# A hybrid attention and SwiGLU layer: the down projection's items parted in pairs with twelve raw slots, its last product in PSUM banks of its own

## The chip, the cores and the metric

The kernel runs on one core of one Trainium2 chip. The metric is the device time of one execution in microseconds, the median of several. An engine is named as the profile names it: PE does matrix products, DVE (VectorE) and ACT (ScalarE) elementwise work, POOL (GpSimd) some more of it, SP issues DMAs.

## The reference

One decoder layer on 512 tokens of width 1024, all in float32: a mixer (forgetting attention and sliding window attention, gated and merged), a layer norm, a SwiGLU feed forward of inner width 2816, a second layer norm.

```python
h = layer_norm(alpha * x + mixer(x), ln1_g, ln1_b)
hid = silu(h @ w_gate) * (h @ w_up)          # 512 x 2816
out = layer_norm(alpha * h + hid @ w_down, ln2_g, ln2_b)
```

What is computed here is the last line: a product of 512 x 2816 by 2816 x 1024, added to alpha times the residual, and then normalised over the 1024 channels of each token.

## The kernel before

Every float32 operand is split into a high part (a rounded float32r copy, made by ACT) and a low part (the rest, raw minus high, made by DVE), and each product is three matmuls: high by high, high by low, low by high. The weights of all stages but the last come in 94 slabs of 128x1024. The feed forward's slabs end at slab 94 (`slab_done` counts them), and PE goes straight on to the down projection.

The down projection is one level of a Strassen-like scheme: seven half-size products instead of eight, in the order M5, M1, M3, M6, M2, M7, M4 (`PRODUCTS`, L82). Each product is 11 items (`PAIRS`), so there are 77, numbered 0 to 76; items 55 to 65 are M7 and 66 to 76 are M4. An item takes a 128x256 piece of the activations (`parts`, summed by POOL) and a 128x512 piece of the weights (`wdn`, or `tw` where POOL had made sums of weights ahead). Its way through the engines:

- SP loads the weights into one of four slots of `raw` (L463), once DVE has finished the item four before (`item_ready`).
- ACT makes the high parts: `ah` (128x256, L824), which waits until PE is through with the item eight before (`item_done`, a ring of eight, `RING`), and `sh` (128x512, L826), which waits for the load.
- DVE makes the low parts `al` and `sl` (both L857 by the helper `low`), and counts `item_ready`.
- PE does two blocks of 128 tokens, three matmuls each (L1709 to L1711). With two blocks in turn an item takes PE six matmuls. `item_done` counts after the second block.

Sums of products stay in PSUM: a bank pair BX takes M1, M6, M7 and M4 one on top of the other, BZ M5 and M3, BY M2. What the output needs of them on the way is added to the residual `res` by DVE (`into_residual`, called by `take_bank` and `take_product`; L1297 and L1299), at the item six after the product's end. M4 may go on top of M7 only when DVE has read BX for M7, and PE waits for that (`bank_taken`, 11 + b). M7's last four items and M4's items go block by block (`items_by_block`), so that the first block of each is done earlier (`block0_done`).

The second layer norm goes by blocks of 128 tokens, k = 4 to 7. Blocks 4 and 5 need no M7 and M4 and are normalised by DVE in between the items from item 62 on (`step` in DVE's loop: statistics and variance, the root's start and the first centring, the rest of the root and the second centring, two scalings). ACT takes the square root (`rstd_root`, L694) in its own order behind item 63 and item 68. Blocks 6 and 7 follow after the last item: block 6 while PE does the second block of M4, block 7 behind the last matmul.

All these orders are written out by hand, engine by engine; each engine does its list in order.

Of the kernel before, what the change touches and what calls it, by code (L numbers as in the profile page):

```python
# [24 lines left out]
ALU = mybir.AluOpType  # L25
# [52 lines left out]
BX, BY, BZ = 4, 6, 2  # L78
# [4 lines left out]
            (A22, True, T4, BX, False))  # L83
# [3 lines left out]
DN_RAW = 4  # L87
# [87 lines left out]
def program(nc, xT, x, slabs, vk_slabs, wdn, rope, rope_tok, sel, b_forget, sinks, ln1_g, ln1_b, ln2_g, ln2_b, out):  # L175
    ctx = ExitStack()
    with ctx:
# [16 lines left out]
        al = at("al", 8, [P, RING, 2 * P], F32R)  # L194
        sg = at("sg", 16, [P, 2, SEQ])
# [207 lines left out]
        def item_raw(e):  # L403
            return raw[:, e % DN_RAW * 512:(e % DN_RAW + 1) * 512]

        def item_slot(ring, e):
            return ring[:, item_offset(e):item_offset(e) + 512]
# [4 lines left out]
        def _(sp):  # L412
# [41 lines left out]
            for e in range(ITEMS):  # L454
                p, i = divmod(e, PAIRS)
                _, summed, w, _, _ = PRODUCTS[p]
                if e == 0:
                    sp.wait_ge(t_stored, 16 * PAIRS)
                if e < DN_RAW:
                    sp.wait_ge(lo_ready, ready(N_DN - 2) + e // 2)  # L460
                else:
                    sp.wait_ge(item_ready, e - DN_RAW + 1)
                sp.dma_start(item_raw(e), (tw if summed else wdn)[i, w]).then_inc(item_landed[e % DN_RAW], 16)  # L463
# [105 lines left out]
        def _(act):  # L569
# [238 lines left out]

            def item_split(e):

                p, i = divmod(e, PAIRS)
                if e == 0:
                    act.wait_ge(t_stored, 16 * PAIRS)
                if p == M5:
                    act.wait_ge(part_made, 3 * i + 1)
                if e == M1 * PAIRS:
                    act.wait_ge(part_made, 3 * PAIRS)
                if p == M3:
                    act.wait_ge(s3_made, i + 1)
                if e < RING:  # L820
                    act.wait_ge(slab_done, N_DN - SPL + 1 + e // 2)
                else:
                    act.wait_ge(item_done, e - RING + 1)
                act.activation(ah[:, e % RING, :], item_part(e), ACT.Copy)  # L824
                act.wait_ge(item_landed[e % DN_RAW], 16 * (e // DN_RAW + 1))
                act.activation(item_slot(sh, e), item_raw(e), ACT.Copy).then_inc(item_hi, 1)  # L826

            for r in range(4):
                if r % 2:
                    f = FT - 2 + r // 2  # L830
                    act.wait_ge(ff_done, f - 1)
                    silu(f)
                item_split(2 * r)
                item_split(2 * r + 1)
            for e in range(RING, ITEMS):
                item_split(e)
# [8 lines left out]
        def _(dve):  # L845
# [457 lines left out]
            def take_bank(p, b):  # L1303
# [25 lines left out]
            for r in range(4):  # L1329
# [3 lines left out]
                item_low(2 * r + 1)  # L1333
            for e in range(RING, ITEMS):
                item_low(e)
                if e <= M7 * PAIRS + RING - 2 and e % PAIRS == RING - 2 and e > PAIRS:
                    take_product(e // PAIRS - 1)
                if e == M4 * PAIRS + 3:
                    dve.wait_ge(block0_done, 1)
                    take_bank(M7, 0)  # L1340
                    dve.wait_ge(item_done, PAIRS * (M7 + 1))
                    take_bank(M7, 1)
                    for k in (TB + 2, TB + 3):
                        taken_statistics(k, 1, 9 + k - TB)
                for k in (TB, TB + 1):
# [11 lines left out]
                    elif step in (3, 4):  # L1357
                        scale(k, step - 3)
            k = TB + 2
            dve.wait_ge(block0_done, 2)  # L1360
            take_bank(M4, 0)
            variance(k, taken_statistics(k, 0, 13))
# [5 lines left out]
            variance(k, taken_statistics(k, 0, 14))  # L1368
# [4 lines left out]
        def _(pe):  # L1373
# [312 lines left out]
            def item(p, i, b):  # L1686
# [10 lines left out]
                if i == 0:  # L1697
# [9 lines left out]
                    elif p == M4:  # L1707
                        pe.wait_ge(bank_taken, 11 + b)
# [5 lines left out]
                elif i == PAIRS - 1 and p in (M7, M4):  # L1714
# [96 lines left out]
```

## Time and profile before

| | |
|---|---|
| median of three runs | 705.03 us (704.56 to 705.15) |
| the profiled execution | 705.2 us |
| its span | 703.4 us, so 1.8 us lie around it |
| PE busy | 689.1 us (98%) |
| DVE busy | 431.3 us (61%) |
| ACT busy | 336.7 us (48%) |
| POOL busy | 141.3 us (20%) |
| span's mean granted clock of PE | 0.996 |

The down projection begins at 586.39 us of the span and its last matmul starts at 695.17 us. Matmuls are pipelined: a matmul's row shows 0.39 us, and the next starts 0.23 us after it. DVE and ACT rows overlap in the same way by 0.1 us or less, so what an instruction costs in a row of them is the distance from start to start.

### The profile page before, as it was taken

How to read it: one execution, taken by the hardware profiler on the slowest of the kernel's cores; microseconds unless marked ns; L12 is line 12 of the kernel's file. 1: busy time of each engine (PE TensorE's matmuls, PEld its weight loads, DVE VectorE, ACT ScalarE, POOL GpSimd, SP SyncE). 2: the span in 40 equal slices, each digit the busy share in tenths (PEclk: the TensorE clock that was granted, in tenths of full speed). 3: DMA queues.
4: the chain of work that ended last, by engine and by line, in shares of the span. 5: the costliest groups of instructions: out<-in, count | busy, mean ns of one | idle time of the engine just before them, and what ended most of it. 6: DMA issues, size and time to landing. Idle time of an engine off the chain costs nothing.

```text
span 703.4 us, 9442 instructions
## 1 busy us (share of the span) xinstructions
PE 689.1 (98%) x3380; PEld 577.2 (82%) x3380; DVE 431.3 (61%) x739; ACT 336.7 (48%) x624; POOL 141.3 (20%) x129
## 2 busy tenths in 40 slices
PE   8999999999999999999999999999999999999985
PEld 6987888888888888888998888888888888888873
DVE  5569997767876236647923442233334337989897
ACT  5678787467766344333223222222222225677741
POOL 2110000000001000000236664355533415100000
PEclk9999999999999999999999999999999999999998
DMA  8221112211114522361357556654466433676643
GB/s 320 78 92 61 61 62 89 90 61 61 61 61 133 226 90 91 114 215 61 102 188 248 210 209 217 230 197 154 161 233 209 149 106 103 184 221 211 187 126 135
DMA packets 34723, 102.09 MB, mean 145 GB/s; under 512 B 3584, under 2 KB 3712, under 8 KB 34688
## 3 DMA queue, kind: packets, MB, share of 16 engines
q1 hardware_dynamic: 27504, 74.36, 31.8%
q0 software_dynamic: 7184, 27.27, 11.7%
q8 instruction: 20, 0.33, 0.2%
q14 instruction: 15, 0.12, 0.1%
HBM read 87.99 MB, written 13.63 MB: 144 GB/s over the span
## 4 chain that ended last, share of the span: by engine, by line
PE 88%; DVE 5%; ACT 3%; issue 1%; DMA 1%; POOL 0%; SPq 0%; DVEq 0%
PE ps L1376 22%; PE ps L1378 22%; PE ps L1377 22%; PE ps L1709 4%; PE ps L1711 4%; PE ps L1710 4%; PE ps L1458 2%; PE ps L1444 2%; PE ps L1414 1%; ACT rope L593 1%; DVE sl L857 1%; PE ps L1409 1%; DMA x_raw<-in_xT 1%; PE ps L1419 1%; DVE sl L849 1%
## 5 line engine op out<-in xcount | busy, mean ns | idle before, releaser
L857 DVE TENSOR_TENSOR sl<-raw,sh 128x512 fp32r<-128x512 f32 (+1 forms) x113 | 111.8, 989 | 77.2 <-ACT sh L807 77.2
L1376 PE MATMUL ps<-hTh,sh 128*128 128x512 f32 x320 | 124.5, 389 | 0.0
L1377 PE MATMUL ps<-hTh,sl 128*128 128x512 f32 x320 | 124.5, 389 | 0.0
L1378 PE MATMUL ps<-hTl,sh 128*128 128x512 f32 x320 | 124.5, 389 | 0.0
L807 ACT ACTIVATE sh<-raw 128x1024 fp32r<-128x1024 f32 x36 | 38.2, 1062 | 146.3 <-PE ps L1378 127.6
L849 DVE TENSOR_TENSOR sl<-raw,sh 128x1024 fp32r<-128x1024 f32 x50 | 61.8, 1236 | 54.7 <-ACT sh L577 54.5
L1376 PE MATMUL ps<-xh,sh 128*128 128x512 f32 x208 | 83.7, 403 | 0.0
L1378 PE MATMUL ps<-xl,sh 128*128 128x512 f32 x208 | 81.3, 391 | 0.0
L1377 PE MATMUL ps<-xh,sl 128*128 128x512 f32 x208 | 81.1, 390 | 0.0
L577 ACT ACTIVATE sh<-raw 128x1024 fp32r<-128x1024 f32 x50 | 52.8, 1058 | 42.8 <-PE ps L1378 36.4
L1378 PEld LDWEIGHTS ps<-hTl,sh 128*128 128x128 f32 x320 | 60.1, 188 | 12.6
L1377 PEld LDWEIGHTS ps<-hTh,sl 128*128 128x128 f32 x320 | 60.1, 188 | 12.5
L1376 PEld LDWEIGHTS ps<-hTh,sh 128*128 128x128 f32 x320 | 60.1, 188 | 12.3
L1709 PE MATMUL ps<-sh,ah 128*128 128x512 f32 x154 | 60.6, 393 | 2.7 <-DVE res L1297 1.9
L1711 PE MATMUL ps<-sl,ah 128*128 128x512 f32 x154 | 59.9, 389 | 0.0
L1710 PE MATMUL ps<-sh,al 128*128 128x512 f32 x154 | 59.9, 389 | 0.0
L826 ACT ACTIVATE sh<-raw 128x512 fp32r<-128x512 f32 x77 | 48.2, 625 | 24.4 <-DMA raw<-in_wdn 13.6
L1378 PEld LDWEIGHTS ps<-xl,sh 128*128 128x128 f32 x208 | 39.0, 188 | 8.5
L857 DVE TENSOR_TENSOR al<-parts,ah 128x256 fp32r<-128x256 f32 x77 | 36.0, 467 | 15.9 <-ACT sh L826 15.6
L1377 PEld LDWEIGHTS ps<-xh,sl 128*128 128x128 f32 x208 | 39.2, 188 | 7.0
L1376 PEld LDWEIGHTS ps<-xh,sh 128*128 128x128 f32 x208 | 39.2, 188 | 6.9
L1276 DVE TENSOR_TENSOR parts<-sg,ps 128x512 f32 x18 | 12.4, 688 | 48.0 <-PE ps L1378 48.0
(217 smaller groups left out, 1297.3 us busy)
## 6 DMA issues: line engine op xcount, KB each, us to landing
raw<-in_slabs SPq DMA_DIRECT2D x86, 512.0 KB, 3.3
stage<-in_wdn POOLq DMA_DIRECT2D x11, 1024.0 KB, 9.1
tw<-tsum POOLq DMA_DIRECT2D x11, 1024.0 KB, 5.7
raw<-tw SPq DMA_DIRECT2D x44, 256.0 KB, 2.8
raw<-in_wdn SPq DMA_DIRECT2D x33, 256.0 KB, 2.9
x_raw<-in_xT SPq DMA_DIRECT2D x8, 256.0 KB, 6.1
res<-in_x POOLq DMA_DIRECT2D x1, 2048.0 KB, 8.9
late_raw<-in_slabs SPq DMA_DIRECT2D x4, 512.0 KB, 4.2
```

What stands on the lines that cost most here:

```text
L577: act.activation(slot(sh, n, width_of(n)), raw_of(n), ACT.Copy).then_inc(hi_ready, 1)
L807: act.activation(slot(sh, m), raw_of(m), ACT.Copy).then_inc(hi_ready, 1)
L826: act.activation(item_slot(sh, e), item_raw(e), ACT.Copy).then_inc(item_hi, 1)
L849: dve.tensor_tensor(slot(sl, n, w), raw_of(n), slot(sh, n, w).bitcast(F32), ALU.subtract).then_inc(lo_ready, 1)
L857: return dve.tensor_tensor(dst, src, hi.bitcast(F32), ALU.subtract)
L1376: pe.matmul(dst, lh, rh, start=start, stop=False)
L1377: pe.matmul(dst, ll, rh, start=False, stop=False)
L1378: return pe.matmul(dst, lh, rl, start=False, stop=stop)
L1444: last = pe.transpose(ps[:, 5 + col // 512, col % 512:col % 512 + P], prob[:, off + (kb - k0) * P:off + (kb - k0 + 1) * P], ident[:, :])
L1709: pe.matmul(dst, lh, rh, start=start, stop=False, skip_group_check=True)
L1710: pe.matmul(dst, ll, rh, start=False, stop=False, skip_group_check=True)
L1711: last = pe.matmul(dst, lh, rl, start=False, stop=stop, skip_group_check=True)
```

## The change

Four things, all in the down projection.

- Items are split in pairs (0 and 1, 2 and 3, ...). ACT makes `ah` of both in one instruction and `sh` of both in one; DVE the same for `al` and `sl`. Where a pair straddles two products (10 and 11, 32 and 33, 54 and 55) `ah` and `al` stay separate. A pair's first instruction waits for all that both items need, and its semaphores count by two. Item 76 is alone.
- The raw weights get twelve slots: the four of `raw` and eight in a new tile `dn_raw` at 32 KB, where the transposed hidden input lay, free once slab 94 is done. From item 20 on a load waits for the item twelve before.
- M4 starts fresh in banks of its own (BW = 0), so PE waits for no bank there. M7's bank pair is therefore added to the residual twice per block (subtracted on the right half, added on the left), and M4's is added to the left half: two more DVE instructions in all. M7 is taken at item 72, like every product at the item six after its end. It was taken at item 69 before.
- M7's last four items and M4's first four go block by turn again, and only M4's last seven block by block. The statistics of the right halves of blocks 6 and 7 move from behind item 69 to behind the last item.

Its core (waits of the loads and the ACT side's order behind the pair are as described):

```diff
-BX, BY, BZ = 4, 6, 2
+BX, BY, BZ, BW = 4, 6, 2, 0
 ...
-            (A22, True, T4, BX, False))
+            (A22, True, T4, BW, True))
-DN_RAW = 4
+DN_RAW = 12
+        dn_raw = at("dn_raw", 32, [P, 8 * 512])
 ...
+        def raw_slot(e):
+            return 8 + e % 4 if e < 8 else (e - 8) % DN_RAW
 ...
-                if e < DN_RAW:
+                if e < 4:
                     sp.wait_ge(lo_ready, ready(N_DN - 2) + e // 2)
-                else:
+                elif e < 8:
+                    sp.wait_ge(item_ready, e - 3)
+                elif e == 8:
+                    sp.wait_ge(slab_done, N_DN)
+                elif e >= 8 + DN_RAW:
                     sp.wait_ge(item_ready, e - DN_RAW + 1)
+                elif e >= 16:
+                    sp.wait_ge(item_ready, e - 11)
 ...
             def item_split(e):
+                s = e % RING
+                if e + 1 < ITEMS and one_product(e):
+                    part_free(e, e + 2)
+                    act.activation(ah[:, s:s + 2, :], item_parts(e), ACT.Copy)
 ...
+                count = min(2, ITEMS - e)
+                for m in range(e, e + count):
+                    act.wait_ge(item_landed[raw_slot(m)], 16 * raw_uses(m))
+                act.activation(item_slot(sh, e, count), item_raw(e, count), ACT.Copy).then_inc(item_hi, count)
 ...
             def item_low(e):
-                dve.wait_ge(item_hi, e + 1)
-                low(al[:, e % RING, :], item_part(e), ah[:, e % RING, :])
-                low(item_slot(sl, e), item_raw(e), item_slot(sh, e)).then_inc(item_ready, 1)
+                s = e % RING
+                count = min(2, ITEMS - e)
+                dve.wait_ge(item_hi, e + count)
+                if count == 2 and one_product(e):
+                    low(al[:, s:s + 2, :], item_parts(e), ah[:, s:s + 2, :])
+                else:
+                    for m in range(e, e + count):
+                        low(al[:, m % RING, :], item_part(m), ah[:, m % RING, :])
+                low(item_slot(sl, e, count), item_raw(e, count), item_slot(sh, e, count)).then_inc(item_ready, count)
 ...
                 elif p == M7:
                     into_residual(2 + b, 1, BX + b, ALU.subtract, 1 + b)
+                    into_residual(2 + b, 0, BX + b, ALU.add, 0)
                 else:
-                    into_residual(2 + b, 0, BX + b, ALU.add, 0)
+                    into_residual(2 + b, 0, BW + b, ALU.add, 12 + 2 * b)
 ...
             for e in range(RING, ITEMS):
-                item_low(e)
-                if e <= M7 * PAIRS + RING - 2 and e % PAIRS == RING - 2 and e > PAIRS:
+                if e % 2 == 0:
+                    item_low(e)
+                if e % PAIRS == RING - 2 and e > PAIRS:
                     take_product(e // PAIRS - 1)
-                if e == M4 * PAIRS + 3:
-                    dve.wait_ge(block0_done, 1)
-                    take_bank(M7, 0)
 ...
                     elif p == M7:
                         pe.wait_ge(bank_taken, 7 + b)
-                    elif p == M4:
-                        pe.wait_ge(bank_taken, 11 + b)
 ...
-            for p in range(M7):
+            for p in range(M4):
                 for i in range(PAIRS):
                     items_by_block(p, i, i + 1)
-            for i in range(PAIRS - DN_TAIL):
-                items_by_block(M7, i, i + 1)
-            items_by_block(M7, PAIRS - DN_TAIL, PAIRS)
-            items_by_block(M4, 0, DN_TAIL)
+            for i in range(DN_TAIL):
+                items_by_block(M4, i, i + 1)
             items_by_block(M4, DN_TAIL, PAIRS)
```

DVE's list where the normalisation of block 4 begins, before: L857 is a low part, first that of item 62's weights; L1105 the variance, L1114 to L1128 the root, L1136 a centring, L1154 a scaling.

```order
L857 TENSOR_TENSOR sl<-raw,sh 128x512
L1327 BN_STATS stats<-res 128x6 [waits bank_taken] x2
L1105 BN_AGGR mv<-stats 128x2 [waits ln_part]
L857 TENSOR_TENSOR al<-parts,ah 128x256 [waits item_hi]
L857 TENSOR_TENSOR sl<-raw,sh 128x512
L1114 TENSOR_SCALAR rstd<-mv 128x1 [waits ln_var,ln_right,ln_left]
L1136 SCALAR_TENSOR_TENSOR res<-res,mv,ln2p 128x512 [waits ln2_landed]
L857 TENSOR_TENSOR al<-parts,ah 128x256 [waits item_hi]
L857 TENSOR_TENSOR sl<-raw,sh 128x512
L1120 RECIPROCAL rstd<-rstd 128x1 [waits ln_root]
L1123 TENSOR_SCALAR rstd<-rstd 128x1 [waits ln_half,ln_rec]
L1136 SCALAR_TENSOR_TENSOR res<-res,mv,ln2p 128x512 [waits ln2_landed]
```

The same place of the changed kernel, from the low part of the pair of items 62 and 63 (its weights). L900 is the low part, L1157 to L1171 the root, L1179 the centring, L1197 the scaling.

```order
L900 TENSOR_TENSOR sl<-dn_raw,sh 128x1024
L1377 BN_STATS stats<-res 128x6 [waits bank_taken] x2
L1148 BN_AGGR mv<-stats 128x2 [waits ln_part]
L1157 TENSOR_SCALAR rstd<-mv 128x1 [waits ln_var,ln_right,ln_left]
L1179 SCALAR_TENSOR_TENSOR res<-res,mv,ln2p 128x512 [waits ln2_landed]
L900 TENSOR_TENSOR al<-parts,ah 128x512 [waits item_hi]
L900 TENSOR_TENSOR sl<-raw,sh 128x1024
L1163 RECIPROCAL rstd<-rstd 128x1 [waits ln_root]
L1166 TENSOR_SCALAR rstd<-rstd 128x1 [waits ln_half,ln_rec]
L1179 SCALAR_TENSOR_TENSOR res<-res,mv,ln2p 128x512 [waits ln2_landed]
L1171 TENSOR_SCALAR rstd<-rstd 128x1 [waits ln_newton]
L1197 SCALAR_TENSOR_TENSOR res<-res,rstd,ln2p 128x512 [waits ln_rstd,ln_centred_l]
```

The low part that stood between the variance and the root's start is gone into the pair ahead of them, and the root's last step is now followed by the scaling that needs it.

DVE's list where M7 is taken, before: it begins at item 69's low part; L1297 adds or subtracts a bank to the residual.

```order
L857 TENSOR_TENSOR al<-parts,ah 128x256 [waits item_hi]
L857 TENSOR_TENSOR sl<-raw,sh 128x512
L1297 TENSOR_TENSOR res<-res,ps 128x512 [waits bank_taken,block0_done]
L1297 TENSOR_TENSOR res<-res,ps 128x512 [waits bank_taken,item_done]
L1327 BN_STATS stats<-res 128x6 [waits bank_taken] x2
L1120 RECIPROCAL rstd<-rstd 128x1 [waits ln_root]
L1123 TENSOR_SCALAR rstd<-rstd 128x1 [waits ln_half,ln_rec]
```

And in the changed kernel, from the pair of items 72 and 73 to that of 74 and 75. L1346 and L1348 are the four additions of M7's banks.

```order
L900 TENSOR_TENSOR al<-parts,ah 128x512 [waits item_hi]
L900 TENSOR_TENSOR sl<-dn_raw,sh 128x1024
L1346 TENSOR_TENSOR res<-res,ps 128x512 [waits bank_taken,item_done]
L1348 SCALAR_TENSOR_TENSOR res<-res,ps 128x512 [waits ln_left]
L1346 TENSOR_TENSOR res<-res,ps 128x512 [waits bank_taken]
L1348 SCALAR_TENSOR_TENSOR res<-res,ps 128x512 [waits ln_left]
L900 TENSOR_TENSOR al<-parts,ah 128x512 [waits item_hi]
L900 TENSOR_TENSOR sl<-dn_raw,sh 128x1024
```

The taking moved from behind item 69 to behind item 73, and went from two instructions to four; the statistics (L1327) that followed it are not here any more.

PE's list at the first matmuls of M4, before (ahead of them the second block of M7's last items):

```order
L1709 MATMUL ps<-sh,ah 128x512
L1710 MATMUL ps<-sh,al 128x512
L1711 MATMUL ps<-sl,ah 128x512
L1709 MATMUL ps<-sh,ah 128x512 [waits bank_taken,item_ready]
L1710 MATMUL ps<-sh,al 128x512
L1711 MATMUL ps<-sl,ah 128x512
L1709 MATMUL ps<-sh,ah 128x512 [waits item_ready]
```

The same rows of the list in the changed kernel:

```order
L1752 MATMUL ps<-sh,ah 128x512
L1753 MATMUL ps<-sh,al 128x512
L1754 MATMUL ps<-sl,ah 128x512
L1752 MATMUL ps<-sh,ah 128x512 [waits item_ready]
L1753 MATMUL ps<-sh,al 128x512
L1754 MATMUL ps<-sl,ah 128x512
L1752 MATMUL ps<-sh,ah 128x512
```

The wait for the bank is gone, and PE waits for the parts of an item (`item_ready`) at every other block, since the two blocks of an item now follow each other.

## Rows read from the trace of the kernel before

**Rows 1.** Page, part 4: shares of the chain that ended last, by engine

```profile
PE 88%; DVE 5%; ACT 3%; issue 1%; DMA 1%; POOL 0%; SPq 0%; DVEq 0%
```

**Rows 2.** Waits by engine, 655 to 703.4 us: total, times, longest (us)

```profile
ACT sh L826 <- DMA raw<-tw: 6.3, 7, 2.3
...
PE ps L1709 <- DVE res L1297: 1.9, 1, 1.9
```

**Rows 3.** Timeline, PE, from 586 us: start us, us, engine line op

```profile
586.39 0.39 PE L1709 MATMUL ps<-sh,ah 128*128 128x512 f32 x1
...
675.93 0.39 PE L1711 MATMUL ps<-sl,ah 128*128 128x512 f32 x1
678.19 0.47 PE L1709 MATMUL ps<-sh,ah 128*128 128x512 f32 x1 [1.88 <-DVE res L1297]
...
689.83 0.50 PE L1709 MATMUL ps<-sh,ah 128*128 128x512 f32 x1 [0.87 <-DVE sl L857]
...
695.17 0.39 PE L1711 MATMUL ps<-sl,ah 128*128 128x512 f32 x1
```

**Rows 4.** Timeline, ACT, 660 to 667 us

```profile
660.03 0.42 ACT L824 ACTIVATE ah<-parts 128x256 fp32r<-128x256 f32 x1 [0.42 <-PE ps L1711]
...
665.84 0.40 ACT L824 ACTIVATE ah<-parts 128x256 fp32r<-128x256 f32 x1
666.15 0.62 ACT L826 ACTIVATE sh<-raw 128x512 fp32r<-128x512 f32 x1
666.68 0.40 ACT L824 ACTIVATE ah<-parts 128x256 fp32r<-128x256 f32 x1
```

**Rows 5.** Timeline, DVE, 661.9 to 671.5 us

```profile
661.95 1.28 DVE L1297 TENSOR_TENSOR res<-res,ps 128x512 f32<-128x512 f32 x2
663.14 0.42 DVE L857 TENSOR_TENSOR al<-parts,ah 128x256 fp32r<-128x256 f32 x1
...
664.08 1.28 DVE L1327 BATCH_NORM_STATS2 stats<-res 128x6 f32<-128x512 f32 x2
...
665.52 0.37 DVE L857 TENSOR_TENSOR al<-parts,ah 128x256 fp32r<-128x256 f32 x1
...
666.41 0.15 DVE L1114 TENSOR_SCALAR rstd<-mv 128x1 f32<-128x1 f32 x1
...
667.14 0.42 DVE L857 TENSOR_TENSOR al<-parts,ah 128x256 fp32r<-128x256 f32 x1
...
668.07 0.15 DVE L1120 RECIPROCAL rstd<-rstd 128x1 f32<-128x1 f32 x1
...
669.24 0.42 DVE L857 TENSOR_TENSOR al<-parts,ah 128x256 fp32r<-128x256 f32 x1
...
670.17 0.75 DVE L1154 SCALAR_TENSOR_TENSOR res<-res,rstd,ln2p 128x512 f32<-128x512 f32 x1
670.83 0.42 DVE L857 TENSOR_TENSOR al<-parts,ah 128x256 fp32r<-128x256 f32 x1
```

**Rows 6.** Timeline, DVE, item 76's last low part, and two rows of block 6

```profile
689.09 0.69 DVE L857 TENSOR_TENSOR sl<-raw,sh 128x512 fp32r<-128x512 f32 x1
...
694.40 0.21 DVE L1128 TENSOR_SCALAR rstd<-rstd 128x1 f32<-128x1 f32 x1
694.71 0.75 DVE L1154 SCALAR_TENSOR_TENSOR res<-res,rstd,ln2p 128x512 f32<-128x512 f32 x1
```

**Rows 7.** Timeline, ACT and DVE, one 128x1024 weight slab

```profile
532.19 1.06 ACT L807 ACTIVATE sh<-raw 128x1024 fp32r<-128x1024 f32 x1 [3.89 <-PE ps L1378]
...
533.29 1.23 DVE L857 TENSOR_TENSOR sl<-raw,sh 128x1024 fp32r<-128x1024 f32 x1 [0.30 <-ACT sh L807]
```

**Rows 8.** Timeline, DVE and POOL, 590 to 602 us

```profile
593.58 0.95 DVE L857 TENSOR_TENSOR al<-parts,ah 128x256 fp32r<-128x256 f32 x1
...
595.60 0.95 DVE L857 TENSOR_TENSOR al<-parts,ah 128x256 fp32r<-128x256 f32 x1
...
590.28 10.93 POOL L563 TENSOR_TENSOR parts<-parts 128x256 f32<-128x256 f32 x11
```

More of the change, by code:

```diff
@@ L401, in item_part, with raw_uses, item_raw, item_slot @@
             return parts[:, i, PRODUCTS[p][0] * 2 * P:(PRODUCTS[p][0] + 1) * 2 * P]
[L403 to L407, printed above, removed]
+        def raw_slot(e):
+            return 8 + e % 4 if e < 8 else (e - 8) % DN_RAW
+        def raw_uses(e):
+            if e < 8:
+                return e // 4 + 1
+            return (e - 8) // DN_RAW + (3 if raw_slot(e) >= 8 else 1)
+        def item_raw(e, count=1):
+            r = raw_slot(e)
+            if r >= 8:
+                return raw[:, (r - 8) * 512:(r - 8 + count) * 512]
+            return dn_raw[:, r * 512:(r + count) * 512]
+        def item_slot(ring, e, count=1):
+            return ring[:, item_offset(e):item_offset(e) + 512 * count]
+        def item_parts(e):
+            p, i = divmod(e, PAIRS)
+            return parts[:, i:i + 2, PRODUCTS[p][0] * 2 * P:(PRODUCTS[p][0] + 1) * 2 * P]
+        def one_product(e):
+            return e // PAIRS == (e + 1) // PAIRS
         block = ctx.enter_context(nc.Block())
@@ L807, in _, with part_free @@
                     act.activation(slot(sh, m), raw_of(m), ACT.Copy).then_inc(hi_ready, 1)
-            def item_split(e):
[L811 to L821, printed above, removed]
-                else:
[L823 to L826, printed above, removed]
+            def part_free(e, end):
+                for e in range(e, end):
+                    p, i = divmod(e, PAIRS)
+                    if e == 0:
+                        act.wait_ge(t_stored, 16 * PAIRS)
+                    if p == M5:
+                        act.wait_ge(part_made, 3 * i + 1)
+                    if e == M1 * PAIRS:
+                        act.wait_ge(part_made, 3 * PAIRS)
+                    if p == M3:
+                        act.wait_ge(s3_made, i + 1)
+                    if e < RING:
+                        act.wait_ge(slab_done, N_DN - SPL + 1 + e // 2)
+                    else:
+                        act.wait_ge(item_done, e - RING + 1)
@@ new lines, in item_split @@
+            def item_split(e):
+                s = e % RING
+                if e + 1 < ITEMS and one_product(e):
+                    part_free(e, e + 2)
+                    act.activation(ah[:, s:s + 2, :], item_parts(e), ACT.Copy)
+                else:
+                    part_free(e, e + 1)
+                    act.activation(ah[:, s, :], item_part(e), ACT.Copy)
+                    if e + 1 < ITEMS:
+                        part_free(e + 1, e + 2)
+                        act.activation(ah[:, s + 1, :], item_part(e + 1), ACT.Copy)
+                count = min(2, ITEMS - e)
+                for m in range(e, e + count):
+                    act.wait_ge(item_landed[raw_slot(m)], 16 * raw_uses(m))
+                act.activation(item_slot(sh, e, count), item_raw(e, count), ACT.Copy).then_inc(item_hi, count)
@@ L1358, in _ @@
                         scale(k, step - 3)
+            for k in (TB + 2, TB + 3):
+                taken_statistics(k, 1, 11 + 2 * (k - TB - 2))
             k = TB + 2
-            dve.wait_ge(block0_done, 2)
+            dve.wait_ge(block0_done, 1)
             take_bank(M4, 0)
-            variance(k, taken_statistics(k, 0, 13))
+            variance(k, taken_statistics(k, 0, 15))
             centre_both(k)
@@ L1367, in _ @@
             take_bank(M4, 1)
-            variance(k, taken_statistics(k, 0, 14))
+            variance(k, taken_statistics(k, 0, 16))
             centre_both(k)
@@ L1713, in item @@
                     last.then_inc(item_done, 1)
-                elif i == PAIRS - 1 and p in (M7, M4):
+                elif i == PAIRS - 1 and p == M4:
                     last.then_inc(block0_done, 1)
```

12 lines of the change are left out of this document (4 added, 8 removed).

## The prediction

> **What bounds the kernel now.** First the chain of waits that ended last, in shares by engine: 88% of it is PE [rows 1]. Nothing that another engine does counts unless it makes PE wait or lies behind its last matmul. Second, PE's timeline over the down projection: do its matmuls follow each other without a hole? The first starts at 586.39, and the last of item 65 at 675.93, after which the next could start 0.23 later, at 676.16. That is 89.77 us for 66 items, 1.36 us an item, 0.68 a block, with nothing lost. All 77 items would end at 586.39 + 77 x 1.36 = 691.11. The last matmul starts at 695.17, so they end at 695.40 [rows 3]. PE lost 4.29 us, all behind item 65. That is the most the change can win here: 705.03 - 4.3 = 700.7.
>
> Third, who PE waited for. 2.03 of the 4.29 go at M4's first matmul (676.16 to 678.19), where DVE had not yet read M7's bank [rows 2, 3]. The other 2.26 lie between 678.2 and 690.6, in small steps at the blocks of M4's last seven items, each released by a low part from DVE, the largest at 689.83 [rows 3]. In that part PE takes a new item every 0.68 us and DVE needs 0.94 for one (663.14 to 664.08) [rows 5]. Fourth, therefore, DVE's timeline: from 661.95 on it does the takings and the normalisation of blocks 4 and 5 between the items [rows 5].
>
> **The change, part by part.** Prices are distances from start to start.
>
> The bank wait goes: 2.03 us, with certainty, since M4 has its own banks. But a wait that goes only counts if the next item is ready. What is late next is DVE's low part, so DVE's list has to be walked through.
>
> Prices for that. An instruction on 128x512 costs 0.60 (two takings, 661.95 to 663.14, make 1.19). A 128x1024 low part lasts 1.23 in its row [rows 7]. A row on 128x512 lasts 0.75 while the next starts after 0.66, an overhang of 0.09 [rows 5], so it costs 1.14. A pair then costs 0.60 + 1.14 = 1.74, against 2 x 0.94 = 1.88 before, 0.14 saved. The bounds of that term: 1.88 if joining saves nothing; below, 256 columns more cost 0.60 - 0.34 = 0.26 and a pair has six times 256, so 1.56 if the fixed part vanished altogether. I take 1.74, the nearest row. On ACT the pair's activations take 0.53, as a 128x512 copy does (666.15 to 666.68) [rows 4], and DVE starts 1.10 after the 128x1024 copy does (532.19 to 533.29) [rows 7].
>
> The walk, from the last point that PE sets in both kernels. ACT's copy at 660.03 waited for item 53's end [rows 4] (586.39 + 54 x 1.36 = 659.83, and the last row's overhang). Before, that released item 61. Now it releases the pair 60 and 61, since a pair needs the ring free for its second item. DVE starts at 660.03 + 0.53 + 1.10 = 661.66. Pair 60/61 to 663.40 (item 61 alone was done at 661.95 [rows 5]). M2's takings 1.19: 664.59. Pair 62/63: 666.33. Statistics and variance 1.44 (664.08 to 665.52 [rows 5]): 667.77.
>
> Here a new hole opens. ACT takes the root only after the variance, and copies after that: before, its next copy stood 0.32 behind the variance's end (665.52 to 665.84 [rows 4, 5]). Before, item 63 filled DVE in this gap and item 64 alone came soon. Now items 64/65 reach DVE at 667.77 + 0.32 + 0.53 + 1.10 = 669.72, and DVE has only the root's start and a centring for that time, 0.73 (666.41 to 667.14 [rows 5]). About 1.0 us of DVE is idle in its busiest stretch.
>
> Pair 64/65: 671.46. Rest of the root with a centring 1.17 (668.07 to 669.24): 672.63. The scaling 0.66 (670.17 to 670.83 [rows 5]) now follows the root's last step at once and waits for it: in block 6 that step and the scaling lie 0.31 apart, against a row of 0.21 that others overlap [rows 6]; I put 0.12 on it: 673.41. Pair 66/67: 675.15. Scaling: 675.81. Statistics of block 5: 677.25. Pair 68/69: 678.99. Its root and centrings in one piece, 0.73 + 1.17: 680.89. Pair 70/71: 682.63. Two scalings: 683.95. Pair 72/73: 685.69. M7's takings, four where there were two, 4 x 0.60: 688.09. Pair 74/75: 689.83.
>
> PE's side. A low part's start and the matmul it releases are 0.74 apart (689.09 [rows 6] to 689.83 [rows 3]), which is 0.60 and 0.14. So PE can start item 74 at 689.97. Without any wait it would have got there at 586.39 + 70 x 1.36 + 4 x 0.68 = 684.31. It has 5.66 us of waits up to this point, spread over items 68 to 74, the largest (over 2 us) at item 74 behind M7's takings. From there it has three blocks of the first and seven of the second kind: 10 x 0.68, and 0.13 for the restart (689.83 to 695.40 is 8 x 0.68 + 0.13 [rows 3]), end at 696.90. Against 695.40: **1.5 us later**. In one sentence: PE resumes for the last time at about the same moment as before, but with ten blocks to do instead of eight.
>
> The rest of the change. Item 76 and the moved statistics end by 689.83 + 0.94 + 1.20 = 691.97, before or at the first block's end (about 692.1), so block 6 fits into the second block's 4.76 us as before; if not, some tenths. The loads: eight start at slab 94 instead of one by one behind DVE, and from item 20 on each has twelve items' time, 16 us; ACT waited 6.3 us for loads in the last 48 us before [rows 2], and that goes. It gains nothing by itself, as DVE's list above never waits for a load. Behind the last matmul nothing changes: one addition, block 7, the store.
>
> POOL's eleven sums, 10.93 us from 590.28, slow DVE: an item's low parts cost 2.02 instead of 0.94 (593.58 to 595.60) [rows 8], 0.54 for each of two instructions. If it is by instruction, a pair costs 1.74 + 1.08 = 2.82 against PE's 2.72: harmless in seven pairs with some 3 us in hand. If it grows with size, a pair costs 4.04 and item 10 is ready at about 586.39 + 0.2 + 1.63 + 3 x 4.04 = 600.3 and a restart later, against 600.0: up to 0.6 us late, which goes straight through: PE is shifted by it. I take the first, at nothing, since 0.54 is the same for both sizes within the sum.
>
> Sum against the profiled execution: span 703.4 + 1.5 = 704.9, and the 1.8 around it, 706.7; its time was 0.2 above the median, so 705.03 + 1.5 = **706.5**.
>
> A rule that speaks against the change: the Trainium skill (Perfetto Trace Analysis, Optimizing Scalar/DVE Operations) says that grouping into larger operations helps where the engine is saturated, but where Scalar or Vector are not saturated and yet cause bubbles elsewhere, breaking instructions up lets work be done sooner. Its first half would make the change a gain of 0.14 a pair, its second half a loss of a pair's delay. DVE here is both, full behind 661.95 and with gaps ahead of it; the rows give the delay (1.45 us at pair 60/61) as larger than the eight savings of 0.14.
>
> **Rivals.** *The waits simply go* (chance 0.12): M7's bank wait was 2.03, the loads kept ACT waiting 6.3 us, both are cured, and PE loses little: between 700.7 and 703.4, say 702.3. For it: both waits stand in the profile by name. Against: DVE has no hole between 661.95 and item 73's low parts, so there is little for faster loads to fill. It decides if DVE has item 74 ready more than 3 us earlier than reckoned, that is with no hole at the root and M7's takings beside something.
>
> *Joining saves more than the rows say* (0.21): a pair costs 1.60, and eight of them give back 1.1 us; the loss and the gain cancel, 705.4.
>
> *POOL's contention grows with size* (0.10): item 10 late, 706.5 + 0.6 = 707.1, with PE holes near 600.
>
> *The forecast* (0.55), by its own bounds 705.8 (pairs at 1.66) to 707.6 (pairs at 1.88). The other 0.02: eight loads at once delay item 8, or PE's clock falls in the holes.
>
> **How the numbers follow.** About 0.2%, 1.4 us, is what a measurement of this kernel can tell from no change: 703.6 and 706.4 are the borders. Faster: the first rival, 0.12. Within: the second, 0.21, and 0.15 of the forecast's 0.55, whose lower part ends below 706.4: 0.36. Slower: 0.40 of the forecast, 0.10 and 0.02: 0.52. The range, 703.4 to 708.4, leaves out most of the first rival below and a forecast that errs together with the third above. The forecast's own range is 705.8 to 707.6.
>
> **What would show it.** No PE wait at M4's first matmul for a bank, but waits for DVE's low parts at items 68, 70, 72 and, the longest, 74, over 5 us together. ACT never waiting for a load behind 620. DVE with one hole of about 1 us behind the first centring near 668.7, and full from there to item 76. Low parts on 128x1024 at 1.23. Last matmul start at about 696.7. Wrong if PE's holes sum to less than 4.3 us, if item 74's low parts end before 688, or if PE waits between 590 and 620.

## The result, and the profile after

The changed kernel takes 707.2 us, the median of ten runs (705.57 to 709.8). The kernel before, beside it on the same chip, takes 705.04 (704.56 to 706.66). The ratio is 1.003, with a 95% interval of 1.002 to 1.0039: about 2.2 us slower. The profiled execution is the fastest of the ten: 705.57 us, with a span of 703.8. So it shows the change at its mildest, which turns out to matter.

The chain of waits by engine, part 4 of the page of the changed kernel, answers to [rows 1]:

```profile
PE 88%; DVE 5%; ACT 3%; issue 2%; DMA 1%; POOL 0%; DVEq 0%; SPq 0%; ACTq 0%
```

PE is still the bound. Its waits, and those it hangs on, from 655 to 703.8 us (total, times, longest), against [rows 2]:

```profile
ACT rstd L721 <- DVE mv L1148: 20.0, 4, 11.0
...
PE ps L1752 <- DVE sl L900: 4.5, 3, 2.5
DVE al L900 <- ACT sh L869: 3.8, 4, 1.1
ACT ah L859 <- PE ps L1754: 3.4, 3, 1.1
```

ACT's 6.3 us for loads are gone and so is PE's 1.9 for a bank. In their place PE waits 4.5 for low parts. PE's timeline, against [rows 3]. This execution reaches the first item's matmul at 585.39, the one before at 586.39, so times are compared from there:

```profile
678.17 0.50 PE L1752 MATMUL ps<-sh,ah 128*128 128x512 f32 x1
...
681.80 0.50 PE L1752 MATMUL ps<-sh,ah 128*128 128x512 f32 x1 [0.61 <-DVE sl L900]
...
684.86 0.50 PE L1752 MATMUL ps<-sh,ah 128*128 128x512 f32 x1 [1.40 <-DVE sl L900]
...
688.99 0.50 PE L1752 MATMUL ps<-sh,ah 128*128 128x512 f32 x1 [2.47 <-DVE sl L900]
...
695.68 0.39 PE L1754 MATMUL ps<-sl,ah 128*128 128x512 f32 x1
```

Items 68, 70, 72 and 74 start late. From the first item's matmul to the last matmul's start is 695.68 - 585.39 = 110.29 us. Before it was 695.17 - 586.39 = 108.78. I call this the stretch; it grew by 1.51. The span grew only from 703.4 to 703.8, since the first item came 1.00 earlier here. Over the fourteen traces of this document that moment lies between 585.39 and 586.39, and it differs by 0.46 even between single_items and single_late, whose programs are the same up to there. So the stretch, and not the span, is compared between traces. Item 74 would have started at 585.39 + 97.92 = 683.31 without waits, and starts 5.68 late.

DVE's timeline, against [rows 5 and 6]:

```profile
660.70 0.69 DVE L900 TENSOR_TENSOR al<-parts,ah 128x512 fp32r<-128x512 f32 x1 [0.89 <-ACT sh L869]
661.31 1.22 DVE L900 TENSOR_TENSOR sl<-dn_raw,sh 128x1024 fp32r<-128x1024 f32 x1
662.45 1.28 DVE L1346 TENSOR_TENSOR res<-res,ps 128x512 f32<-128x512 f32 x2
...
667.11 0.74 DVE L1179 SCALAR_TENSOR_TENSOR res<-res,mv,ln2p 128x512 f32<-128x512 f32 x1
668.74 0.69 DVE L900 TENSOR_TENSOR al<-parts,ah 128x512 fp32r<-128x512 f32 x1 [0.89 <-ACT sh L869]
...
671.53 0.21 DVE L1171 TENSOR_SCALAR rstd<-rstd 128x1 f32<-128x1 f32 x1
671.84 0.75 DVE L1197 SCALAR_TENSOR_TENSOR res<-res,rstd,ln2p 128x512 f32<-128x512 f32 x1
...
684.73 0.68 DVE L1346 TENSOR_TENSOR res<-res,ps 128x512 f32<-128x512 f32 x1
...
686.52 0.68 DVE L1348 SCALAR_TENSOR_TENSOR res<-res,ps 128x512 f32<-128x512 f32 x1
687.12 0.68 DVE L900 TENSOR_TENSOR al<-parts,ah 128x512 fp32r<-128x512 f32 x1
687.72 1.22 DVE L900 TENSOR_TENSOR sl<-dn_raw,sh 128x1024 fp32r<-128x1024 f32 x1
688.85 0.42 DVE L900 TENSOR_TENSOR al<-parts,ah 128x256 fp32r<-128x256 f32 x1
```

A pair takes 0.61 + 1.14 = 1.75. DVE is done with pair 60/61 at 662.45, stands idle for 0.97 before 668.74, is full from there, and gives 2.39 us to four takings of M7 (684.73 to 687.12) before the last pair.

### The profile page after: what moved, and what is told of

The parts are those of the page before. It is cut to its first block, busy times and chain, and to the rows that moved or that the text cites. A ratio compares the mean times of both kernels' runs of the same rounds, so it can differ in the third digit from the quotient of the medians.

```text
span 703.8 us, 9359 instructions
## 1 busy us (share of the span) xinstructions
PE 688.6 (98%) x3380; PEld 577.4 (82%) x3380; DVE 429.0 (61%) x668; ACT 327.0 (46%) x551; POOL 144.8 (21%) x129
## 4 chain that ended last, share of the span: by engine, by line
PE 88%; DVE 5%; ACT 3%; issue 2%; DMA 1%; POOL 0%; DVEq 0%; SPq 0%; ACTq 0%
PE ps L1421 22%; PE ps L1423 22%; PE ps L1422 22%; PE ps L1752 4%; PE ps L1753 4%; PE ps L1754 4%; PE ps L1503 2%; PE ps L1489 2%; DVE sl L900 1%; PE ps L1459 1%; PE ps L1454 1%; ACT rope L620 1%; PE ps L1464 1%; DMA first_raw<-in_slabs 1%; DVE sl L892 1%
## 5 line engine op out<-in xcount | busy, mean ns | idle before, releaser
L900 DVE TENSOR_TENSOR sl<-raw,sh 128x1024 fp32r<-128x1024 f32 (+1 forms) x51 | 76.3, 1497 | 76.9 <-ACT sh L834 76.9
L900 DVE TENSOR_TENSOR al<-parts,ah 128x512 fp32r<-128x512 f32 (+1 forms) x42 | 30.5, 732 | 23.8 <-ACT sh L869 23.8
L859 ACT ACTIVATE ah<-parts 128x512 fp32r<-128x512 f32 x35 | 22.1, 631 | 44.2 <-PE ps L1754 29.2
```

The costliest lines, as they stand in the source:

```text
L859: act.activation(ah[:, s:s + 2, :], item_parts(e), ACT.Copy)
L900: return dve.tensor_tensor(dst, src, hi.bitcast(F32), ALU.subtract)
```

## The experiments

Each was timed beside the kernel before, in three groups. The median of before was 705.00 in the first (again, slots_only, single_items, late_take), and on another chip 705.29 in the second (banks_only, single_late, mixed_late, filled) and 705.39 in the third (pairs_to_61, root_later, two_takings, before_filled). So between groups ratios to before are compared, not times. A ratio's 95% interval is about 0.001 to each side, 0.6 to 0.8 us. The theory: DVE's list sets the end of the down projection, by three delays (joining at pair 60/61, the hole at the root, two more takings ahead of the last pair), and the loads are worth nothing. What it did not cover at first is why the median is 2.2 us above before and the stretch only 1.5. The interval of the ratio begins at 1.4 us, so this 0.7 is itself uncertain.

**again**: the changed kernel, unchanged.

> The changed kernel as it is, once more, for its spread and a second trace. Its median was 2.2 us above before, 0.7 us more than the 1.5 us that its own trace shows between the first item and the last matmul (110.29 against 108.78 us). Theory A (the whole loss lies in the down projection, the rest is scatter of the first 15 us, where the loads of the input arrive): the stretch from the first item's matmul to the last matmul is 110.3 us again within 0.3, and the median stands 1.0 to 2.2 above before. Rival (the change costs something more, in the stretch too, in some executions): the stretch differs by over 0.5 from the first trace.

707.53 us (706.34 to 708.15), ratio 1.0033 (1.0021 to 1.0045). The second trace, timeline of PE behind the last hole:

```profile
689.19 0.50 PE L1752 MATMUL ps<-sh,ah 128*128 128x512 f32 x1 [2.47 <-DVE sl L900]
...
690.26 0.63 PE L1752 MATMUL ps<-sh,ah 128*128 128x512 f32 x1
690.68 0.63 PE L1753 MATMUL ps<-sh,al 128*128 128x512 f32 x1
...
692.82 0.51 PE L1752 MATMUL ps<-sh,ah 128*128 128x512 f32 x1
693.16 0.39 PE L1753 MATMUL ps<-sh,al 128*128 128x512 f32 x1
...
697.50 0.39 PE L1754 MATMUL ps<-sl,ah 128*128 128x512 f32 x1
```

and PE in windows of the same trace (from:to, length, busy and matmuls, granted clock, DMA share, GB/s):

```profile
685.00:690.00 5.00, 2.47 (x9) 0.96 0.00 0
690.00:692.00 2.00, 2.00 (x7) 0.50 0.00 0
692.00:694.00 2.00, 2.00 (x8) 0.73 0.00 0
```

The holes are the same (0.61, 1.40, 2.47), but behind the last one the granted clock is 0.50, the 1.2 GHz level, for some 3 us. Seven steps from matmul to matmul are 0.43 instead of 0.23, and the two around them 0.1 too long: 7 x 0.2 + 0.2 = 1.6 us. The stretch is 697.50 - 585.60 = 111.9, so 1.6 longer. In the first trace all these windows have 1.00. So the rival was right here: the change costs more in some executions, in the stretch itself, by the clock behind the holes. The medians agree with that as the source of the 0.7 us, though a second trace alone doesn't prove it; filled tests it below.

**slots_only**: before, with twelve raw slots.

```diff
-DN_RAW = 4
+DN_RAW = 12
```

> The kernel before with the twelve raw slots alone: items one at a time, M4 on top of M7 with its bank wait. Theory (DVE bounds the end, loads cost PE only the one hole ahead of item 76): ACT waits for no load behind 600 us, the bank wait stays at about 1.9, holes behind it shrink by 0.9: time 0.9 below before, stretch 107.9. Rival (the load waits of 6.3 us were a cause of their own): 2 us or more below before. Second rival (loads were hidden anyway): same as before.

704.39 us (703.62 to 705.14), 0.9988 (0.9978 to 0.9998). The stretch is 108.23, 0.55 shorter than before. What went is before's hole of 0.87 ahead of item 76 [rows 3], where ACT had waited 0.93 for item 76's load (ACT's timeline of before):

```profile
688.08 0.63 ACT L826 ACTIVATE sh<-raw 128x512 fp32r<-128x512 f32 x1 [0.93 <-DMA raw<-tw]
```

The bank's hole is still there, and the clock is lowered behind it (PE's timeline, then a window, then DVE's timeline at item 76):

```profile
678.08 0.63 PE L1725 MATMUL ps<-sh,ah 128*128 128x512 f32 x1 [1.88 <-DVE res L1313]
...
680.64 0.63 PE L1725 MATMUL ps<-sh,ah 128*128 128x512 f32 x1
681.07 0.63 PE L1726 MATMUL ps<-sh,al 128*128 128x512 f32 x1
```

```profile
680.00:685.00 5.00, 5.00 (x20) 0.84 0.15 56
```

```profile
688.08 0.68 DVE L873 TENSOR_TENSOR sl<-raw,sh 128x512 fp32r<-128x512 f32 x1
```

Eight steps of 0.43 from 678.08 to 681.50 make about 1.6 us of lost clock, yet the stretch is only 0.3 above the 107.9 expected. DVE starts item 76's low part at 688.08, so PE, 0.74 later as in before, could not have begun that item ahead of 688.82, however fast its matmuls; it began at 689.30. Most of what PE lost was time in which it would have waited for DVE. Slow matmuls cost their full length only if no such wait follows them.

**single_items**: the changed kernel with items one at a time (twelve slots, own banks, four takings stay). **banks_only**: the same with four slots.

```diff
+SIZE = {e: 1 for e in range(ITEMS)}
 ...
-                count = min(2, ITEMS - e)
+                count = SIZE[e]
```

> The changed kernel with items parted one at a time; twelve slots, M4's own banks and the four takings stay. Theory (pairs cost: the delay of a pair, the hole at the root, and two more blocks behind the last low part): walked through with the prices of the trace, PE's last low parts come one by one, holes of about 2.5 us at item 73 behind M7's takings and small ones after, last matmul 2.3 us earlier than in the changed kernel: stretch 107.9 us, time 0.9 us below before. Rival (the two more takings are the cause, pairs help by 0.14 each): 0.5 to 1 us above the changed kernel, stretch about 111.

> The changed kernel with items one at a time and four raw slots: M4's own banks, the four takings and the new block order alone. Theory (with own banks the loads aren't on DVE's path): the same as the single kernel with twelve slots, 704.5, hole of 2.3 to 2.5 at item 73. Rival (the loads then set the last items, as they did before the change ahead of item 76): 0.5 to 1.5 us more than that.

704.47 (703.43 to 706.64), 0.9992 (0.9984 to 1.0001), and 704.78 (703.8 to 705.91), 0.9993 (0.9984 to 1.0002). The stretches are 109.0 and 109.03. Each has a single hole, at item 73, the first behind M7's takings here (PE's timeline of the first, its window, and DVE's low part of item 76):

```profile
685.61 0.50 PE L1757 MATMUL ps<-sh,ah 128*128 128x512 f32 x1 [2.30 <-DVE sl L903]
```

```profile
685.00:690.00 5.00, 4.39 (x11) 0.66 0.00 0
```

```profile
687.68 0.68 DVE L903 TENSOR_TENSOR sl<-raw,sh 128x512 fp32r<-128x512 f32 x1
```

The walk gave 107.9 for the first. The trace agrees: DVE starts item 76's low part at 687.68, so PE could begin that item at 688.42, and eight blocks and a restart behind it the last matmul would start at 693.76, a stretch of 107.9. The other 1.1 us is the clock behind the hole (0.66). Two things follow. With banks of their own for M4, slots are worth nothing that these intervals show. And joining, the only thing left out, is what costs: without it the other edits are not measurably slower than before.

**pairs_to_61**: pairs for items 0 to 61, one at a time after.

```diff
+SIZE = {e: 2 if e < 62 else 1 for e in range(ITEMS) if e >= 62 or e % 2 == 0}
```

> The changed kernel with pairs only for items 0 to 61, before the normalisation, and single items from 62 on. M4's own banks, twelve slots and four takings stay. Theory (a pair's delay at the point where DVE becomes the bound costs most): item 61's low parts end 1.45 us later than with single items, and this is never made up: stretch 109.4 us in an execution that keeps its clock, 1.4 above the single kernel's 107.9 without clock loss; median 705.5 to 706.2, the single kernel's being 704.5. Rival (only the pairs during the normalisation cost, by the hole at the root and the late last items): same as the single kernel.

706.26 (705.04 to 707.12), 1.0011 (1.0002 to 1.002), stretch 110.15. PE's timeline:

```profile
682.50 0.50 PE L1757 MATMUL ps<-sh,ah 128*128 128x512 f32 x1 [0.27 <-DVE sl L903]
...
684.10 0.50 PE L1757 MATMUL ps<-sh,ah 128*128 128x512 f32 x1 [0.64 <-DVE sl L903]
...
687.43 0.80 PE L1757 MATMUL ps<-sh,ah 128*128 128x512 f32 x1 [2.37 <-DVE sl L903]
```

It differs from single_items only in how DVE comes into its busy part, one pair against single items. The hole at 687.43 is again ahead of item 73, which starts 687.43 - 586.18 = 101.25 behind the first item, against 685.61 - 585.87 = 99.74: 1.51 later, ahead of any lowered clock. That is the delay at pair 60/61, predicted as 1.45, and it is never made up. The stretch shows 1.15 of it, since single_items lost 1.1 to the clock behind its hole and pairs_to_61, by the same reckoning from its item 76, 0.75. The ratios show 1.3, with 0.9 to each side.

**root_later**: ACT's roots and DVE's root steps each a pair later, so that a pair stands in the hole.

```diff
+STEPS = {62: ((4, 0),), 63: ((4, 1),), 66: ((4, 2), (4, 3)), 67: ((4, 4), (5, 0)), 68: ((5, 1),),
+         70: ((5, 2),), 71: ((5, 3), (5, 4))}
 ...
-                    if e == M7 * PAIRS + RING + 5 * (k - TB):
+                    if e == M7 * PAIRS + RING + 2 + 4 * (k - TB):
```

> The changed kernel with ACT's square roots one pair later (behind items 65 and 69) and DVE's rest of the root behind items 67 and 71: pairs throughout. Theory (DVE's hole of about 0.9 us between the first centring and pair 64/65 goes, since ACT splits 64/65 before it takes the root): stretch 109.4 us, 0.8 to 0.9 below the changed kernel in an execution that keeps its clock; median 0.5 to 1 below it. Rival (the hole only absorbs what DVE would wait for later): stretch 110.3.

706.62 (704.99 to 707.38), 1.002 (1.0012 to 1.0029). DVE's timeline has no hole now:

```profile
667.33 0.74 DVE L1181 SCALAR_TENSOR_TENSOR res<-res,mv,ln2p 128x512 f32<-128x512 f32 x1
667.98 0.69 DVE L902 TENSOR_TENSOR al<-parts,ah 128x512 fp32r<-128x512 f32 x1
```

The stretch is 109.51, 0.8 shorter where the hole was 1.0. PE's timeline shows why the clock has no part in the difference:

```profile
685.67 0.63 PE L1753 MATMUL ps<-sh,ah 128*128 128x512 f32 x1
686.10 0.63 PE L1754 MATMUL ps<-sh,al 128*128 128x512 f32 x1
...
688.43 0.50 PE L1753 MATMUL ps<-sh,ah 128*128 128x512 f32 x1 [1.27 <-DVE sl L902]
```

The clock falls behind the hole of 1.97 ahead of item 72 (0.72 in the window from 685), but item 74 waits for DVE after that, and starts 688.43 - 585.60 = 102.83 behind the first item against 103.60. DVE is 0.77 earlier and not 0.97, since the second root's last step is now followed by its scaling too and waits for it, 0.31 where it took 0.13. By ratio the kernel is 0.7 us below the changed one, inside the expected 0.5 to 1, but the two intervals overlap, and it stays above before. The delay exists; curing it alone doesn't undo the loss.

**two_takings**: M7's banks are added to only one half, which leaves two additions out of the result.

```diff
-                    into_residual(2 + b, 0, BX + b, ALU.add, 0)
```

> The changed kernel without the two additions of M7's banks to the left half of the residual (that part of the sum is left out). Theory (each instruction of DVE ahead of the last pair costs its 0.60 in full): stretch 109.1 us, 1.2 below the changed kernel in an execution that keeps its clock, hole at item 74 of 1.3 instead of 2.5; median 1.0 to 1.8 below it. Rival (they lie in DVE's slack): same as the changed kernel.

704.75 (704.05 to 706.8), 0.9994 (0.9985 to 1.0002). PE's timeline at item 74, and stretch 109.11:

```profile
688.08 0.50 PE L1751 MATMUL ps<-sh,ah 128*128 128x512 f32 x1 [1.27 <-DVE sl L900]
```

Two takings are 1.20, and the hole went from 2.47 to 1.27, as expected. The median went down by more than the 1.0 to 1.8 expected, 0.36% or 2.5 us against the changed kernel (0.9 to each side). The granted clock of this trace stays 1.00. That a hole half as long costs less than half would fit; with one trace it isn't shown.

**late_take**: the changed kernel with M7's takings behind item 76.

```diff
-                if e % PAIRS == RING - 2 and e > PAIRS:
+                if e % PAIRS == RING - 2 and e > PAIRS and e // PAIRS - 1 != M7:
 ...
+            take_product(M7)
```

> The changed kernel with M7's four takings moved from behind item 73 to behind item 76. Theory (DVE's list is the bound and what is moved behind the last low part comes back ahead of block 6): PE's hole at item 74 falls from 2.5 to about 0.3 and its last matmul comes 2.4 us earlier (stretch 107.9), but block 6's normalisation then starts 2.0 us after its block is done and block 7's waits for it: only 0.5 us below the changed kernel. Rival (PE's last matmul sets the end): 2.4 us below the changed kernel.

705.74 (705.19 to 706.16), 1.0008 (0.9999 to 1.0017). PE keeps the two small holes (0.61 and 1.40) and the clock; the stretch is 107.91, 2.4 shorter. Yet the span is 703.8, as in the changed kernel's trace: from the last matmul's start to the span's end it is now 9.93 us instead of 8.12, since DVE, with the takings still to do, sets the end, and the other 0.6 is a later first item (585.96). So 1.8 of the 2.4 us came back behind PE. By ratio the kernel is 1.6 us below the changed one, more than the expected 0.5, and its eleven executions lie within 1.0 us: the hole at item 74, behind which the clock could fall, is gone.

**single_late**: late_take with single items. **mixed_late**: the same, but pairs for items 66 to 73 alone, in DVE's full part, where each saves 0.14.

```diff
+SIZE = {e: 2 if 66 <= e < 74 else 1 for e in range(ITEMS) if not (66 <= e < 74 and e % 2)}
```

> The same with every item alone. Theory: 0.6 us above the mixed kernel (four pairs save 0.14 each), 1.0 below before, clock at 1.00 and a narrow spread, while the kernel with single items and the takings at item 72 had a hole of 2.3 us, a granted clock of 0.66 behind it and stood only 0.5 below before. Rival (the place of the takings doesn't matter in the single kernel, since DVE sets the end in both): same median as that kernel, 704.5.

> The changed kernel with items one at a time, pairs only from item 66 to 73, where ACT is ahead and a pair delays nothing, and M7's takings behind item 76. Theory (DVE's list sets the end, PE holes over some 1.5 us also cost clock in some executions): PE has one hole of about 0.3 us, its clock stays at 1.00, the last matmul comes at a stretch of about 105 us, DVE ends the kernel: 1.5 us below before in the walk, and 1.5 to 2.3 in the median, since before has a hole of 1.88 that can cost clock. Rival (holes don't matter, PE's last matmul sets the end): 4 us below before. Second rival (takings behind item 76 cost more than they give, as in the run with pairs): same as before.

703.97 (703.28 to 704.3), 0.9981 (0.9972 to 0.999), and 703.42 (702.58 to 704.95), 0.9979 (0.9969 to 0.9989). The traces list no wait of PE for DVE in either. Mixed_late's windows (same columns) are all but full until its last matmul, and its stretch is 104.94, hardly more than 77 x 1.36 = 104.72; single_late's is 105.51, so four pairs save 0.57, about 4 x 0.14, though the two times can't be told apart:

```profile
680.00:685.00 5.00, 4.93 (x22) 1.00 0.28 105
685.00:690.00 5.00, 5.00 (x23) 1.00 0.00 0
690.00:692.00 2.00, 0.74 (x4) 1.00 0.00 0
```

Of 3.84 us of stretch saved against before, 1.5 (by ratio) to 1.9 (by medians) remain in the time, since part of block 6 and block 7 now wait for DVE behind the last matmul: from its start to the span's end it is 700.7 - 690.35 = 10.35 us, against 703.4 - 695.17 = 8.23 before. Both versions stand below before with their whole intervals, and so below the changed kernel.

**filled**: the changed kernel, with useless matmuls in the holes.

```diff
+FILL = {M4 * PAIRS + 4: 2, M4 * PAIRS + 6: 5, M4 * PAIRS + 8: 10}
 ...
+                    for _ in range(FILL.get(e, 0)):
+                        pe.matmul(ps[:, BY, :], ah[:, (e - 1) % RING, 0:P], item_slot(sh, e - 1), start=True, stop=True,
+                                  skip_group_check=True)
                     pe.wait_ge(item_ready, e + 1)
```

> The changed kernel with matmuls of no use put into PE's three last holes: two ahead of item 70, five ahead of 72, ten ahead of 74, into a bank that nothing reads any more, all shorter than the holes. The output's work is unchanged. Theory (in some executions the granted clock falls behind the holes and the last blocks go at 0.43 us a matmul, which is the 0.7 us between the trace's 1.5 and the median's 2.2, and the wide spread): stretch 110.3 us in every execution, clock 1.00 to the last matmul, median 0.5 to 1.0 below the changed kernel and spread under 1.5 us. Rival (scatter comes from the first 15 us): same median and spread as the changed kernel.

705.92 (705.55 to 706.78), 1.0013 (1.0004 to 1.0022). The work is more and items 70, 72 and 74 start as late as without them (item 70 at 682.41, 96.40 behind the first item, against 681.80 - 585.39 = 96.41; item 74 at 103.59 against 103.60). The stretch is 110.3 with the clock at 1.00, and the median is 1.2 us lower than the changed kernel's by ratio (0.9 to each side). The spread is 1.2 us, against 4.2 in the ten executions of the changed kernel and 1.8 in the six of again. What differs is PE's idle time, so some of the changed kernel's time hangs on it: by this run 1.2 us, by the stretch 0.7.

**before_filled**: the same for before, eight ahead of M4's first matmul and three ahead of item 76.

```diff
+                        for _ in range(8):
+                            pe.matmul(ps[:, BY, :], lh, rh, start=True, stop=True, skip_group_check=True)
```

> The kernel before with matmuls of no use in its holes: eight ahead of M4's first matmul, where PE waits for the bank, three ahead of item 76. The output's work is unchanged. Theory (before too loses clock behind its hole of 1.9 us in some executions): 0.3 to 0.8 us below before, stretch 108.8 us. With it the loss by the walk alone can be read between two kernels that keep their clock: the filled changed kernel (705.92) should stand 1.5 above this one, so 704.4. Rival (before loses no clock): same as before, and the two stand 0.6 to 0.9 apart.

705.51 (704.35 to 706.52), 1.0003 (0.9994 to 1.0012), stretch 108.95. I expected 0.3 to 0.8 below before; nothing came. The rival, that before loses next to nothing by the clock, fits, and slots_only shows a likely reason: behind the bank's hole DVE sets the pace and slow matmuls cost little. No trace of before itself has a lowered clock there, so this is argued. Filled should then stand 1.35 to 1.5 above this kernel (the stretches are 110.30 and 108.95), and by ratio it stands 0.7 above, with 0.9 to each side. So the two don't contradict each other, and they don't settle the size either.

## Why the prediction was right, and which term was mis-sized

706.5 was predicted, 707.2 measured, inside the range and slower by over 0.2% as the likeliest case had it. The forecast's 1.5 us is not met by luck: the steps that it is made of came out one by one.

- *The bank wait goes, low parts take its place*: shown in the trace of after (no wait for a bank, 4.5 us for low parts).
- *The walk*: from ACT's copy for pair 60/61 (ACT's timeline of the changed kernel, against [rows 4])

```profile
659.09 0.63 ACT L859 ACTIVATE ah<-parts 128x512 fp32r<-128x512 f32 x1 [1.14 <-PE ps L1754]
```

  to PE's end I had 36.87 us. In the trace it is 695.68 + 0.23 - 659.09 = 36.82. The takings ahead of the last pair, 2.39 against 2.40, and the start of item 74 (5.68 behind an unhindered PE against 5.66) came out as reckoned. "1.5 us later" is 1.51 between the two traces.
- *The delay at pair 60/61*: 1.45 reckoned, 1.51 between pairs_to_61 and single_items at item 73.
- *A pair costs 1.74*: 1.75. The rival that joining saves more falls, and so does the one that the waits simply go.
- *The loads gain nothing*: banks_only and single_items agree within 0.0001 in ratio. In the old order of the blocks and banks they were worth something: slots_only has a stretch 0.55 shorter and a ratio just below 1, since item 76's load came late before.
- *The hole at the root*: 0.97 against 1.0; root_later closed it and had item 74 start 0.77 earlier.
- *The scaling waits for the root's last step*: 671.53 to 671.84, 0.31, as reckoned.
- *POOL slows DVE by instruction, not by size*: settled by the trace. Pairs beside POOL's sums, DVE's timeline and POOL's row, against [rows 8]:

```profile
588.45 1.75 DVE L900 TENSOR_TENSOR sl<-raw,sh 128x1024 fp32r<-128x1024 f32 x1
590.14 1.21 DVE L900 TENSOR_TENSOR al<-parts,ah 128x512 fp32r<-128x512 f32 x1
591.28 1.76 DVE L900 TENSOR_TENSOR sl<-dn_raw,sh 128x1024 fp32r<-128x1024 f32 x1
```

```profile
589.21 14.68 POOL L590 TENSOR_TENSOR parts<-parts 128x256 f32<-128x256 f32 x11
```

  The pair takes 591.28 - 590.14 = 1.14 and 592.96 - 591.28 = 1.68, so 0.54 more for either size, 2.82 in all. PE waits for nothing there.
- *PE's clock falls in the holes*: this was the mis-sized term. The prediction named it among "the other 0.02" and gave it no price. In the traces it costs 1.6 us in one execution (again), nothing in another (after), and by the medians 0.7 to 1.2: the changed kernel loses 2.2 where its stretch in the mildest execution loses 1.5, and filled is 1.2 below it. The ten executions of the changed kernel fit: the two slowest (709.43 and 709.8) have the lowest mean granted clock, 0.993, and the two with the highest, 0.998, took 706.54 and 705.88. But the slowest stand 4 us above the traced one, more than the 1.6 that a trace shows, and none of them was traced; what else they lost stays open. The holes could be seen ahead: the change turns small steps of 2.26 in all and one wait of 2.03 into three real holes that grow, 0.61, 1.40 and 2.47, close together, the last with no wait behind it that would take up slow matmuls. Only the trace of before, at 1.00 behind its own hole, spoke for no cost. The Trainium skill (TensorE: Matmul & The Clock Gate, A second HAM failure mode: psum-queue depth-cycling) says that frequent micro-idles between groups of matmuls make the clock swing between its two levels, and that it is the swing that costs throughput. By that sentence the forecast would have been above 706.5, and the traces of again (0.50), root_later (0.72) and pairs_to_61 (0.73) agree that the clock falls, while those of after and two_takings, at 1.00, show that it need not. Single_items (0.66) has but one hole, so it doesn't take several, and in root_later the fall cost nothing.

The Trainium skill (Perfetto Trace Analysis, Optimizing Scalar/DVE Operations) says that breaking instructions up may let work finish sooner where Scalar or Vector aren't saturated but cause bubbles on other engines. The runs bear it out: 0.14 saved a pair, 1.51 us lost by the pair's delay (pairs_to_61 against single_items).

## What to carry to other kernels

Join instructions only where the engine that does them has results in hand; where the bound engine waits for each one, a joined instruction hands over late, here by 1.5 us, more than the 1.1 that eight joined pairs save. Follow the feeding engine's list up to the last thing that the bound engine needs, and put everything else, such as takings of a finished product, behind it, until that engine itself sets the end. Price a hole in PE above its length if no other wait follows it, since the clock may fall behind it; where waits follow, they take up the slow matmuls. Where the work can't be moved, a few idle-time matmuls may hold the time steady, as in filled, or give nothing, as in before_filled.

## What the runs showed of the hardware

- Behind holes of 1.9 to 2.5 us the granted clock fell in some executions to 0.50 for some 3 us (again) or 0.66 to 0.84 over some 5 us behind the hole (single_items, banks_only, root_later, pairs_to_61, slots_only). The same kernel with the same holes kept 1.00 in another execution (after). With the holes filled the spread was 1.2 us, without 4.2 and 1.8.
- Matmuls at the lower clock start 0.43 us apart instead of 0.23. Eight such steps cost the stretch 0.3 us where DVE's low parts set the pace behind them (slots_only), and seven, with a slower one on each side, 1.6 us where nothing did (again).
- A DVE instruction beside POOL's sums lost 0.54 us whether it had 256, 512 or 1024 columns. POOL's eleven sums took longer beside the longer ones: 14.68 us beside pairs and 10.93 beside single items (10.94 in single_items).
